# Decoder step of two layers: keys of four requests scored side by side, with the parts and the convolution interleaved anew

## What is computed

```python
# one new token per request, 16 heads of 96 in 4 key groups, 2048 past positions in pages of 128
s   = q_rot . keys          # window: 512 cached keys; selection: 16 pages = 2048 keys, masked to the chosen blocks
p   = softmax(s * SCALE)
o_sel, o_win = p @ values
# the prompt: 256 x 256 causal scores, once for the selected and once for the window keys, each of 16 heads
o   = gate0 * o_cmp + gate1 * o_sel + gate2 * o_win
c   = silu(layer_norm(conv31(u) + bias))      # depthwise, 31 taps, 512 channels
out = concat(o, c) @ w_out
```

## Time and profile before

| what | value |
|---|---|
| median of 3 runs | 2438.67 us (2437.85 to 2438.88) |
| profiled execution, its own time | 2438.98 us |
| its span, first to last instruction | 2437.1 us |
| PE busy | 2388.9 us (98%) |
| DVE busy | 1474.5 us (61%) |
| ACT busy | 1071.9 us (44%) |
| moved | 516.80 MB, mean 212 GB/s |

### The profile page before, as it was taken

One profiled execution on the slowest core, in us unless ns is written; L12 is line 12 of the kernel. 1 busy time (PEld: TensorE's weight loads), 2 busy tenths in 40 slices (PEclk: granted clock), 3 DMA queues, 4 the chain that ended last, 5 costly groups with the idle time before them and its releaser, 6 DMA issues.

```text
span 2437.1 us, 50797 instructions
## 1 busy us (share of the span) xinstructions
PE 2388.9 (98%) x20548; PEld 2258.7 (93%) x20548; DVE 1474.5 (61%) x1732; ACT 1071.9 (44%) x1302; POOL 94.1 (4%) x180
## 2 busy tenths in 40 slices
PE   8999998999999999999999999999999999999997
PEld 6888862779999999999999999999999999999996
DVE  6777778675866444444444778768754444444456
ACT  3333321454575353354353445446743534433433
POOL 0000014220000000000000010000000000000000
PEclk9999999999999999999999999999999999999998
DMA  9999669895555555555555564454555544454451
GB/s 377 352 327 325 213 202 319 303 332 224 186 188 214 199 213 200 211 202 183 205 178 184 174 227 172 169 175 173 173 188 174 186 176 181 180 181 181 179 184 70
DMA packets 102974, 516.80 MB, mean 212 GB/s; under 512 B 13088, under 2 KB 29536, under 8 KB 56640
## 3 DMA queue, kind: packets, MB, share of 16 engines
q1 hardware_dynamic: 91872, 467.90, 53.8%
q0 software_dynamic: 10976, 47.13, 5.6%
HBM read 508.59 MB, written 18.95 MB: 216 GB/s over the span
## 4 chain that ended last, share of the span: by engine, by line
PE 91%; DVE 4%; ACT 1%; issue 1%; DMA 1%; POOLq 0%; POOL 0%; SPq 0%; ACTq 0%; DVEq 0%
PE psa L441 28%; PE psa L442 27%; PE psa L443 27%; PE psm L477 2%; PE psa L645 1%; ACT whi L1100 1%; PE psm L841 1%; PE psa L820 1%; DVE page L1625 1%; DVE wlo L1609 1%; DVE stage L1835 1%; PE psa L638 1%; PE psm L672 1%; DMA page<-in_cmp 0%; PE psm L829 0%
## 5 line engine op out<-in xcount | busy, mean ns | idle before, releaser
L1609 DVE TENSOR_TENSOR wlo<-wraw,whi 128x2048 fp32r<-128x2048 f32 x356 | 815.7, 2291 | 770.3 <-ACT whi L1100 770.0
L1100 ACT ACTIVATE whi<-wraw 128x2048 fp32r<-128x2048 f32 x356 | 682.1, 1916 | 968.1 <-PE psa L443 962.1
L441 PE MATMUL psa<-xhi,whi 128*128 128x264 f32 (+1 forms) x2096 | 605.3, 289 | 13.7 <-DVE wlo L1609 12.0
L442 PE MATMUL psa<-xlo,whi 128*128 128x264 f32 (+1 forms) x2096 | 600.4, 286 | 0.0
L443 PE MATMUL psa<-xhi,wlo 128*128 128x264 f32 (+1 forms) x2096 | 599.0, 286 | 0.0
L443 PE MATMUL psa<-hhi,wlo 128*128 128x264 f32 x2048 | 581.4, 284 | 0.0
L442 PE MATMUL psa<-hlo,whi 128*128 128x264 f32 x2048 | 581.3, 284 | 0.0
L441 PE MATMUL psa<-hhi,whi 128*128 128x264 f32 x2048 | 580.8, 284 | 0.0
L443 PE MATMUL psa<-nhi,wlo 128*128 128x264 f32 x1536 | 435.2, 283 | 0.0
L442 PE MATMUL psa<-nlo,whi 128*128 128x264 f32 x1536 | 434.9, 283 | 0.0
L441 PE MATMUL psa<-nhi,whi 128*128 128x264 f32 x1536 | 434.9, 283 | 0.0
(11 more groups left out here) (424 smaller groups left out, 1565.2 us busy)
## 6 DMA issues: line engine op xcount, KB each, us to landing
wraw<-in_w SPq DMA_DIRECT2D x356, 1024.0 KB, 4.8
page<-in_cmp SPq DMA_DIRECT2D x128, 384.0 KB, 5.2
kbuf<-in_selk SPq DMA_DIRECT2D x64, 192.0 KB, 4.0
kbuf<-in_selk POOLq DMA_DIRECT2D x64, 192.0 KB, 4.2
vbuf<-in_selv SPq DMA_DIRECT2D x64, 192.0 KB, 4.2
vbuf<-in_selv POOLq DMA_DIRECT2D x64, 192.0 KB, 4.3
o_win<-in_win POOLq DMA_DIRECT2D x8, 1533.0 KB, 7.6
kbuf<-in_wink SPq DMA_DIRECT2D x8, 768.0 KB, 5.4
```

Source lines behind the costliest of these rows:

```text
L441: mm(out, wh, hi[:, k, 0:w], start=(k == 0), stop=False)
L442: mm(out, wh, lo[:, k, 0:w], start=False, stop=False)
L1100: A(whi[:, p % 2, :], wraw[:, p, :], ACT.Copy).then_inc(s.hi_ready, 1)
L1609: V.tensor_tensor(wlo[:, p % 2, :], wraw[:, p, :], whi[:, p % 2, :].bitcast(F32), ALU.subtract).then_inc(s.lo_ready, 1)
```

## The change

- Keys are scored four units at a time: `keys(j)` takes units 4j to 4j+3 in three rounds of four products, each 32 columns wide and each in its own column strip. The order of the requests becomes 0, 2, 4, 6, 1, 3, 5, 7 (`request(u)`). All queries lie in `qzr`; `qzm` and `middle` go.
- The strips then come out in another row order. So ACT copies each finished bank (`rows_copy`, five times) and PE multiplies it with a permutation back into the bank (`turn_keys`, five times); `bank_out` waits for that (`k_turned`). The transposes of the queries (L600) use the same permutation.
- Keys and values share seven slots: the five and two more (`kmore`) in the space of `tsam` and `ckt`. The last three value units use slots 3 to 5 again.
- `block_score`s are interleaved with the query transposes (`queries_and_blocks`).
- The parts begin after `keys(6)` and not after unit 32: units 28 to 39 are scored in parts 1, 3 and 5. Values begin in part 6, with three units in parts 6, 9, 12 and 15 and two in the others.
- Convolution: `taps` becomes `tap_sums(m)` (m rounds of 4 taps, the same instructions). 9 rounds stand ahead of the parts, 22 in parts 0 to 14. `query_rope(2)` and `(3)` move into parts 5 and 11. The convolution's later steps move by one or two parts (13 to 15, 14 to 16, 16 to 18), `bank_out(4)` from part 4 to 7, the turned selection weights from part 6 to 8.

```diff
+        KEYS_AT = {1: 7, 3: 8, 5: 9}
+        SEL_AT = 8
+        SUMS = (2, 2, 1, 1, 1, 1, 1, 1, 2, 2, 1, 2, 2, 2, 1)
+        def value_slots(i):
+            return (2, 1) if i in (6, 9, 12, 15) else (1, 1) if 6 <= i < 24 else (0, 0)
+        def place(u):
+            return u % 7 if u < 77 else u - 74
+        def slot(u):
+            return kbuf[:, place(u), :] if place(u) < 5 else kmore[:, place(u) - 5, :]
+        def request(u):
+            return 2 * (u % 4) + u % 8 // 4
+        def before(u):
+            return max(v for v in range(u) if place(v) == place(u))
...
@@ SP, and POOL alike
-                    sp.wait_ge(s.k_used, u - 4)
+                elif u < 7:
+                    sp.wait_ge(s.cmp_mm, 1)
+                    sp.wait_ge(s.rows_mm, 2)
+                    sp.wait_ge(s.stored, 16 * 6)
+                else:
+                    sp.wait_ge(s.k_used, before(u) + 1)
...
@@ PE
-                if r % 2:
-                    middle(u - 1, (32, 64)).then_inc(s.k_used, 1)
-                    middle(u, (0, 96))
-                for t, lo in ((0, 0), (2, 64)):
-                    last = mm(psa[lo:lo + 64, c % 2, :], qzr[:, r, lo:lo + 64], key[:, :, t, :], start=(r == 0), stop=(r == NB - 1),
-                              skip_group_check=True)
+                for t in rounds:
+                    for n in range(4):
+                        u = 4 * j + n
+                        if t == 0:
+                            pe.wait_ge(kin[place(u)], landed(u))
+                            if u >= 8:
+                                pe.wait_ge(kin_p[place(u)], landed_p(u))
+                        key = slot(u).rearrange("p (q t n) -> p q t n", q=4, t=3)
+                        ins = mm(psa[32 * n:32 * n + 32, c % 2, :], qzr[:, t, e, 32 * n:32 * n + 32], key[:, :, t, :],
+                                 start=(e == 0 and t == 0), stop=(e == 1 and t == 2), skip_group_check=True)
+                        if t == 2:
+                            ins.then_inc(s.k_used, 1)
+            def turn_keys(c):
+                pe.wait_ge(s.k_copied, c + 1)
+                mm(psa[:, c % 2, :], C("perm"), ktmp[:], start=True, stop=True).then_inc(s.k_turned, 1)
...
+            queries_and_blocks(1)
+            turn_keys(0)
+            keys(2)
+            queries_and_blocks(2)
+            compressed_sums()
+            queries_and_blocks(3)
+            keys(3)
+            block_scores(3)
+            compressed_turn()
+            turned_queries(0)
+            turn_keys(1)
+            compressed_output()
+            keys(4)
+            prompt_keys(0)
+            keys(5)
...
+            turn_keys(2)
...
-                    keys(next(key_units))
+                    if 2 <= 2 * g + t < 5:
+                        keys(6, (2 * g + t - 2,))
...
@@ ACT
+            def rows_copy(c):
+                act.wait_ge(s.k_used, 8 * c + 8)
+                if c:
+                    act.wait_ge(s.k_turned, c)
+                A(ktmp[:], psa[:, c % 2, :], ACT.Copy).then_inc(s.k_copied, 1)
...
@@ DVE
-                dve.wait_ge(s.k_used, 8 * c + 8)
+                dve.wait_ge(s.k_turned, c + 1)
...
-            taps(16)
-            query_rope(2)
+            tap_sums(2)
             dve.wait_ge(s.sc_mm, 4)
...
-            taps(8)
-            query_rope(3)
...
-            taps(12)
             bank_out(1)
-            taps(28)
+            tap_sums(3)
             bank_out(2)
...
-                    taps(5)
+                    if t:
+                        tap_sums(1)
...
-                if i < 4:
-                    taps(5)
-                if i == 1:
+                if i < len(SUMS):
+                    tap_sums(SUMS[i])
+                if i in (5, 11):
+                    query_rope(2 + i // 11)
+                if i == 3:
                     bank_out(3)
```

More of the change, by code:

```diff
@@ L206, in part, with landed_p @@
             return g, kind, min(sub, 1), (0, 0, 2)[sub], (4, 2, 2)[sub]
-        def landed(u):
-            return 16 * sum(1 if v < 8 else 2 for v in range(u % 5, u + 1, 5))
+        VALUE0 = 40
+        def place(u):
[4 more added lines that the diff above has]
+            return 2 * (u % 4) + u % 8 // 4
+        def landed(u):
+            return 16 * sum(1 if v % VALUE0 < 8 else 2 for v in range(u + 1) if place(v) == place(u))
+        def landed_p(u):
+            return 32 * sum(1 for v in range(u + 1) if place(v) == place(u) and v % VALUE0 >= 8)
+        def before(u):
+            return max(v for v in range(u) if place(v) == place(u))
         o = Region(region_a, a_yacc)
@@ L616, in _, with keys @@
             group(9, xhi, xlo, None, query_hooks)
[L619 to L625, removed]
+            def keys(j, rounds=(0, 1, 2)):
+                c, e = divmod(j, 2)
+                if j == 0:
                     pe.wait_ge(s.qz_done, 2)
-                if r == 0:
+                if e == 0 and rounds[0] == 0:
                     if c < 2:
@@ L631, in keys @@
                         pe.wait_ge(s.k_evac, c - 1)
[L632 to L640, removed]
@@ L748, in compressed_output @@
                 mm(psm[:, 3, 256:256 + HD], ocs, Pm("wcv", parts=HD), start=True, stop=True).then_inc(s.ocmp_mm, 1)
-            keys(next(key_units))
-            keys(next(key_units))
+            keys(0)
             pe.wait_ge(s.pk_prod, 1)
+            pe.wait_ge(s.imp_read, 1)
             for t in range(2):
@@ L756, in _ @@
                               start=True, stop=True)
-            last.then_inc(s.pk_mm, 1)
-            keys(next(key_units))
-            pe.wait_ge(s.imp_read, 1)
-            plain_queries(0)
-            keys(next(key_units))
+                if t:
+                    last.then_inc(s.pk_mm, 1)
+                flip_queries(0, t, tok[:, t, Q0:Q0 + KW])
+            keys(1)
             pe.wait_ge(s.pk_copied, 1)
@@ L864, in _ @@
                     scores(i)
-                if i < 4:
-                    keys(next(key_units))
-                elif i < 24:
+                if i in KEYS_AT:
+                    keys(KEYS_AT[i])
+                for _ in range(value_slots(i)[0]):
                     values(next(value_units))
+                if i in (2, 6):
+                    turn_keys(3 + i // 6)
                 if 1 <= i <= 24:
@@ L903, in _ @@
                     last.then_inc(s.conv_var, 1)
-                if i < 4:
-                    keys(next(key_units))
-                elif i < 24:
+                for _ in range(value_slots(i)[1]):
                     values(next(value_units))
@@ L1718, in _ @@
             dve.wait_ge(s.rows_copied, 1)
-            V.memset(qzm[:], 0.0)
             step(V.memset(qzr[:], 0.0))
```

253 lines of the change are left out of this document (119 added, 134 removed).

## The result

The changed kernel takes 2456.07 us (median of 4 runs, 2453.75 to 2457.72) against 2438.26 us before (4 runs, 2437.72 to 2438.88): ratio 1.0072, 95% interval 1.0055 to 1.009. It is slower by 17.8 us. The forecast was 2436.5 with a range up to 2446, so both the number and its range missed; "slower" had 0.22. The profiled execution took 2456.1 us with a span of 2454.3.

A forecast was written before the change was run, and what follows sets the result against it. It took DVE's chain of work as the bound up to group 10: waits of 28.1 us against 30.3, plus 1.8 moved behind part 15, make the stretch 2.2 us shorter, hence 2436.5 us, range 2425 to 2446.

The forecast's parts named there:

- Keys on PE: Key scoring: ten groups of three 1.0 us rounds, 30 us instead of 60; permutations add 5; PE relieved of 25.
- DVE's work, 138.0 us up to part 15: From 324.3 to part 15's start: DVE has 138.0 us of work, so part 15 begins at 462.3 plus waits.
- Waits 1 to 3: DVE's waits ahead of the eight products: rank table 2.0 us, block scores 4.2, bank 2 9.2.
- Wait 4, the eight products: DVE's wait among the eight products ahead of the parts: 0.9 us each on PE, 4.6 us of waits in all.
- the clock falls: Rival: relieved PE idles and drops to the slow level, chiefly in parts 9 to 14; 2441 to 2450 us, chance 0.17.
- Wait 5, parts 0 to 14, 8.1: DVE's waits for PE's outputs: 2.6 us in parts 2 and 3, 4.2 in part 8, 1.3 in part 9.
- Behind it 51.0 us as before plus the 1.8: Part 15 to group 10: 51.0 us as before plus 1.8 for mean and subtraction, so group 10 at 543.2.
- Hidden: Value transfers: last unit issued two parts before use, 9 us against 2.3 + 4.2 needed, so it costs nothing.
- the tightest: From 324.3 to group 10: DVE's chain of convolution, query turning, masks and evacuations sets the time, no engine being full.
- part 0 after 400: Sign: part 0 forecast on DVE at 394; wrong if before 388 or after 400.
- a clock of the second window under 0.95: Sign: forecast wrong if PE's clock in the window of the parts, from part 0 to part 15, is under 0.95.
- DVE's waits in parts 0 to 14: Sign: forecast wrong if these waits total under 3 or over 14 us.

The follow-up runs named there:

- c4: The changed kernel with five rounds of taps taken out of parts 8 to 13 and put ahead of bank 2: 2448.0 us.
- e1: The changed kernel with the weights of group 10 held back until the last unit of values has landed: 2452.9 us.
- c1: The kernel before with only the convolution, the two later query turnings and the norm at their new places, keys unchanged: 2462.8 us, ratio 1.0109.
- f1: The kernel before with 64 of the 124 taps left out: 2436.5 us, ratio 0.9995.
- c3: The changed kernel with extra matmuls of constants where PE waited in the key stage: 2450.2 us, ratio 1.0050.
- d4: c3 with extra 512-column matmuls also where PE waits for DVE in parts 6, 12, 19 and 23: 2447.0 us, ratio 1.0044.
- d3: The kernel before with only its norm steps later, at parts 15 to 23 instead of 13 to 22: ratio 1.0008.
- d1: The changed kernel with more tap rounds ahead of block scores and bank 2 and behind the products, fewer in parts, norm at its old parts: ratio 1.0004.
- d2: d1 with the extra matmuls of c3 in PE's waits of the key stage: 2437.5 us, ratio 1.0004.
- g3: e2 with the hold of e1 and 512-column matmuls after five of the eight products: 2432.0 us, ratio 0.9971.
- e2: d2 with three rounds of taps between mask and evacuation of part 8 and fewer in parts 1, 9 and 10: ratio 0.9997.
- g2: d2 with the weights of group 10 held back as in e1: 2436.4 us, ratio 0.9989.

## Why the prediction was wrong, step by step

- *Keys on PE.* Right, and a little better: 24 instructions in 2.78 us, 0.93 a round instead of 1.0. The Trainium skill (TensorEngine Tiling, Key Properties) says that changing the tiling mode drains the engine; the new order changes it less often, and that may be the gain. No run here separates it.
- *DVE's work, 138.0 us up to part 15.* Right to 0.2 us, as the check above shows.
- *Waits 1 to 3.* 3.2, 2.7 and 9.7 against 2.0, 4.2 and 9.2: 0.2 us off in sum. The whole stretch starts 1.0 us later (cprod at 325.1 instead of 324.1), which the prediction did not have. That is no part of the change: in the other executions cprod begins between 323.8 (c4) and 326.3 (e1), with the old keys too (324.9 in c1, 326.1 in f1).
- *Wait 4, the eight products: "Each lasts 0.9".* This step failed: 10.2 against 4.6. Six of the eight, and the rounds of keys(6) among them, ran at 1.2 GHz. c3 shows it: with seven at 2.4 GHz the wait is 4.6. The rival "the clock falls" had this mechanism, but looked for it in parts 9 to 14, where its cost is small (d4), and not here.
- *Wait 5, parts 0 to 14, 8.1.* 12.8, too small by 4.7. Part 8 cost 6.0 instead of 4.2; part 9 3.1 instead of 1.3, since values(8) waits for DVE's own rows behind two rounds of taps (PE idles 3.7 us); parts 2, 3 and 5 cost 3.7, where 2.6 stood for parts 2 and 3.
- *"Behind it 51.0 us as before plus the 1.8."* Failed: 61.1. The late norm costs 3.5 more (d3, and every run with it), the last values 4.7 (e1).
- *The last values "Hidden", 9 us against 2.3 + 4.2.* Failed: 8.2 us from the last issue to landing beside the weights (at most 4.1 with them held back), while the room was 6.
- *Together.* The late start of 1.0, 0.2 in waits 1 to 3, 5.6 in wait 4, 4.7 in wait 5, 0.4 in two waits of 0.2, and 8.3 behind part 15 are 20.2 us; group 10 begins 20.1 us behind the forecast's 543.2.
- *The comparison itself.* The sum set 28.1 us of waits against 30.3 and called the taps' move neutral. c1 shows what that move costs by itself, 1.1%, some 0.1% of it the norm's. It was the largest single cause and none of the rivals: the forecast traded waits in the parts for waits in the keys one for one, by a sum whose terms all had to be right. It took DVE's chain for "the tightest" in the whole stretch. Ahead of the parts it was so by 2 to 4 us only (f1), so DVE's work taken away from there brings little; and in the parts DVE waited 24.1 us while PE had 77.8 of 81.2 us to do. c4 and d1 recover 0.25 and 0.7% by order, 0.1% of the latter by the norm's.

Of its own signs, part 0 after 400 (401.0, by no more than executions differ), a clock of the second window under 0.95 and group 10 more than 53 us behind part 15 all said "wrong"; DVE's waits in parts 0 to 14 stayed inside their bounds.

What stays open: how much of the 17.8 us is the clock's. Alone it is worth 0.2% (c3), on top of the right order nothing (d2), in g3 it may be part of the step below e2. The causes cover each other and do not add.

## What to carry to other kernels

An engine that is a few microseconds from being the bound is filled by the order of its work: before moving work off a stretch, ask what that engine will do there instead, and price the wait, not the work. Relieving an engine (PE by 25 us) is worth what the next bound leaves (here nothing with the old order, 8 to 9 us at part 0 otherwise, in single profiles), and gaps that it opens can slow that engine. When buffers are shared to start a later stage's transfers early, look at the last transfer of the earlier stage. And before reading a step of a few microseconds off two profiles, look how far apart two profiles of the same code are.

## What the hardware showed

Adding matmuls to PE made the kernel faster: the third product took 1.64 us after idle times of 1.34 and 0.65 us, and 0.91 in c3, with one extra matmul in each of those gaps and four in the waits for keys ahead of them. Six short products in d1 (1.64 us each) stay slow, with idle times of 0.72 us and less between them. A transfer of 192 KB took 8.2 us from issue to landing beside 4 MB of weights, and at most 4.1 without them. The level is not fixed by the program alone: d2 and g2 have the same instructions in the key stage, and their profiled executions show a clock of 0.92 and 0.83 in the window from 324.3 to 413.2, with part 0 at 397.5 and 407.0. Such kernels spread by 9 to 13 us over their runs (d1 2434.7 to 2443.6, g2 2430.6 to 2443.4), g3 by 5, the kernel before by 6 to 7.
